# Two blocks of transformer layers in one kernel: another order of small matmuls between the large ones in the second block's mixer

## The chip, the cores and the metric

The kernel runs on one core of a Trainium2 chip. The time is the device time of one execution in microseconds (us), the median of three runs. A profiled execution gives the trace: spans of every instruction on TensorE (PE; its weight loads are shown apart as PEld), VectorE (DVE), ScalarE (ACT), GpSimd (POOL) and the DMA queues (SP).

## The reference

The input x (256 rows of 1024 values) goes through a first block and then a second block of two layers each. Each layer is a feed-forward part, a mixer and a second feed-forward part. Only the second block's mixer is touched. Cut to that:

```python
(z, xbc, dt_raw, rq, rk, rv, rg, aq, ak, av, gate) = jnp.split(h @ w_in[l], offsets, axis=-1)
y_ssd = ssd_mixer(z, xbc, dt_raw, ...)        # 16 heads of 64, chunks of 128 rows
y_ret = retention_mixer(rq, rk, rv, rg, ...)  # 4 heads
y_att = swa_sink_attention(aq, ak, av, ...)   # 16 query heads, 2 key/value heads, band of 256 keys
ys = jnp.stack([y_ssd, y_ret, y_att], axis=2)
branch = jnp.einsum('blmc,mcd->blmd', ys, w_branch[l])
gates = jax.nn.sigmoid((gate + b_gate[l]).reshape(bsz, L, N_BRANCH, D_MODEL))
y = jnp.sum(gates * branch, axis=2) @ w_out[l]

# in ssd_mixer, for each chunk and head j
lmat = jnp.exp(jnp.where(causal, seg, -jnp.inf))                       # the decays
y_diag = jnp.einsum('bcgjls,bcsgjp->bclgjp', cb[:, :, :, None] * lmat, xdt)
# in swa_sink_attention
p = e / (jnp.sum(e, axis=-1, keepdims=True) + jnp.exp(sink - m))
o = jnp.einsum('bnkgqs,bnskd->bnqkgd', p, vb)
```

## The kernel before, in words

Every engine has its own instruction queue, written out by hand in the order in which it executes; between the queues stand semaphores only. Nothing is scheduled by a tool.

**Units.** All weights stream through as units of 128x2048 values (`load`, on SyncE's queue, 5 buffers `raw`). ScalarE's `split` (line 1229) casts a unit to its high part `w_hi` (4 buffers), VectorE's `split` (line 1727) subtracts that and leaves the low part `w_lo`. TensorE's `product` (line 684) multiplies one 128x512 piece three times: high by high, high by low, low by high. One unit is used for both row blocks r = 0 and 1; `part` does one row block with one unit: 4 pieces x 3 = 12 products. The text calls that a half. `half(name, c, q, first, r)` is such a half for column chunk c of a projection, unit q of its two; `both` does r = 0 and 1; `chunk` does two units. Before a half TensorE waits until VectorE has split its unit (`unit_split`), and, where q is 0, until the accumulator pair that it overwrites was read (`chunk_read`, counted for r = 0 and 1 apart). A half that is done frees the unit (`unit_used`). ScalarE and VectorE interleave the splits with their own work by `through(u)`: split all units up to u of this mixer.

**Accumulators.** PSUM has four banks `acc`, used as two pairs (one bank for each row block), and four banks `work`, used in turn. The table `CHUNKS` gives each projection its pair: both chunks of gate_a (`gate_a0`, `gate_a1`) and both chunks of `gate_s` lie in pair 0; `ys`, the outputs of heads 0 to 7 and then of heads 8 to 15, lies in pair 1 both times. A bank of `work` is taken by `fill`, which waits until the last content was read (`work_read`).

**Attention.** For key/value group g and row block r, `attend` makes scores, VectorE masks them and takes maxima (lines 1966 to 1976), ScalarE makes the exponentials (line 1440) and scales them (line 1450), `turn_probs` transposes the four pairs of heads on TensorE into the four `work` banks (`probs_turned`, line 909), ScalarE copies them out (`copy_probs`, line 1467), and `gather` multiplies them with the values (`values`, line 925). Set (1, 0) has one key tile of 128 (8 transposes, 16 small products), set (1, 1) has two (16 and 32). ScalarE's `values_high` (line 1458) reads the result when both row blocks are in it. `add_bias` on VectorE (line 1948) scales a gate chunk from its accumulators, adds the bias and frees the pair.

**SSD heads.** ScalarE's `decays(i)` (lines 1669 and 1674) writes the decays of a group of heads, `HEADS = (0, 3, 6, 9, 12, 14, 16)`, into `seg`, which has six places: head hd uses place hd % 6, and so a group waits until the heads six before it are multiplied (`y_done`). VectorE's `weights` (line 2309) multiplies them with C·B, head by head (`seg_ready`). `weigh(hd)` on TensorE (lines 1181 and 1182) makes the head's output, 64 columns for each of two chunks. `carried` (line 1170) makes the part that comes from the first chunk's state; VectorE's `carry` (lines 2298 and 2301) takes it. VectorE's `skipped(g)` (line 2318) waits for the eight heads of group g, adds the skip and frees pair 1; `outputs(g)` (line 2331) multiplies with z. Beside these, TensorE runs the eight halves of `gate_s` (units 44 to 47).

The orders of ScalarE and VectorE around the heads, which the change does not touch:

```python
# ScalarE
decays(0); through(47); decays(1); decays(2); through(48)
decays(3); decays(4); through(49); gate(... "gate_s", 0 ...); decays(5); through(50)
# in decays(i), before the exponential that writes seg
if end > 6:
    act.wait_ge(y_done, l * 16 + (end - 6))
# VectorE
weights(range(0, 3)); through(47); weights(range(3, 6)); carry(0); carry(1); through(48)
add_bias(... "gate_s", 0 ..., rows=(0,)); weights(range(6, 8)); add_bias(..., rows=(1,))
skipped(0); weights(range(8, 11)); through(49); outputs(0); weights(range(11, 16))
skipped(1); outputs(1); through(50)
```

(The calls are put on fewer lines here, without their other arguments.)

Of the kernel before, what the change touches and what calls it, by code (L numbers as in the profile page):

```python
# [109 lines left out]
def build(nc, a):  # L110
# [3 lines left out]
    half = dm // 2  # L114
# [19 lines left out]
    with ExitStack() as ctx:  # L134
# [541 lines left out]
        def _(pe):  # L676
# [151 lines left out]
            def part(block, l, name, i, q, pos, r, x, kts=4, cols=512, units=2, turn_name=None):  # L828

                pair, n = count("chunks", block, l, name, i)  # L830
                if q == 0:
                    pe.wait_ge(chunk_read[pair], n * 2 - 1 + r)
                slot, nu = unit_count(pos)
                pe.wait_ge(unit_split[slot], nu + 1)
                for t in range(kts):
                    kt = kts * q + t
                    if turn_name and r == 0 and kt % 2 == 0:
                        turned(block, l, turn_name, kt // 2)
                    last = product(x[0], x[1], kt, r, pos, t * cols, cols, acc[2 * pair + r][:, 0:cols],
                                   kt == 0, q == units - 1 and t == kts - 1)  # L840
                last.then_inc(unit_used[slot], 1)
# [35 lines left out]
            def fill(block, l, name, i=0):  # L877

                bank, n = count("work", block, l, name, i)
                pe.wait_ge(work_read[bank], n)  # L880
                return work[bank], work_filled[bank]
# [19 lines left out]
            def probs_turned(block, l, g, r, e):  # L901

                nk = key_tiles(block, r)
                for hp in range(4):
                    bank, filled = fill(block, l, f"probsT{g}{r}", hp)
                    pe.wait_ge(probs_scaled, events(block, l, [8 * n for n in PASSES], 8 * g + 4 * r + hp + 1))
                    for s in range(2):
                        for kt in range(nk):
                            last = nc.tensor.transpose(bank[:, (s * nk + kt) * P:(s * nk + kt + 1) * P],  # L909
                                                       e(g, r, hp)[:, s, kt * P:(kt + 1) * P], ident[:, :])  # L910
                    last.then_inc(filled, 1)

            def values(block, l, g, r, e, v, kv):

                nk = key_tiles(block, r)
                pair, n = count("chunks", block, l, f"pv{g}")
                pe.wait_ge(chunk_read[pair], n * 2)
                for i in range(0, 4, 2):
                    for s in range(2):
                        turned(block, l, f"probsT{g}{r}", i + s)  # L920
                    for j in range(2):
                        for kt in range(nk):
                            for s in range(2):
                                pT = e(g, r, i + s).rearrange("p s n -> p (s n)")
                                last = nc.tensor.matmul(  # L925
                                    acc[2 * pair + i // 2][64 * s:64 * s + 64, j * 256 + r * P:j * 256 + (r + 1) * P],
                                    v[:, kt, kv(i) * 64:kv(i) * 64 + 64], pT[:, (j * nk + kt) * P:(j * nk + kt + 1) * P],
                                    start=kt == 0, stop=kt == nk - 1)
                    last.then_inc(pv_done, 1)
# [77 lines left out]
            def mixer2(l):  # L1007
# [13 lines left out]
                def half(name, c, q, first, r, x=xt, turn_name=None):  # L1021
                    part(1, l, name, c, q, m + first + q, r, x, turn_name=turn_name)

                def both(name, c, q, first, x=xt, turn_name=None):
                    for r in range(2):
                        half(name, c, q, first, r, x, turn_name)
# [34 lines left out]
                def turn_probs(g, r):  # L1061

                    probs_turned(1, l, g, r, B["e"])

                def gather(g, r):

                    values(1, l, g, r, B["e"], B["v"], lambda hp: g)
# [34 lines left out]
                attend(1, 1)  # L1102
                both("br_r", 1, 1, 24, yt)
                both("gate_a0", 0, 0, 26)
                turn_probs(1, 0)
                both("gate_a0", 0, 1, 26)
                gather(1, 0)
                turn_probs(1, 1)
                both("gate_a1", 0, 0, 28)
                gather(1, 1)  # L1110
                both("gate_a1", 0, 1, 28)
                chunk("xbc", 0, 30)
# [52 lines left out]
                def carried():  # L1165

                    pe.wait_ge(scaled_ready, l + 1)
                    for g in range(2):
                        bank, filled = fill(1, l, "mid", g)
                        nc.tensor.matmul(bank[:, :], S["cb"][:, g, 2 * P:3 * P], S["scaled"][:, g * 512:(g + 1) * 512],  # L1170
                                         start=True, stop=True).then_inc(filled, 1)

                def weigh(hd):

                    pair, n = count("chunks", 1, l, "ys", hd // 8)
                    if hd % 8 == 0:
                        pe.wait_ge(chunk_read[pair], n * 2)
                    pe.wait_ge(seg_ready, l * 16 + (hd + 1))
                    c, v = (hd % 8) * 64, slice(hd * 64, hd * 64 + 64)
                    w = S["seg"][:, hd % 6, :]  # L1180
                    nc.tensor.matmul(acc[2 * pair][:, c:c + 64], w[:, 0:P], S["xdt"][:, 0, v], start=True, stop=True)  # L1181
                    nc.tensor.matmul(acc[2 * pair + 1][:, c:c + 64], w[:, P:2 * P], S["xdt"][:, 1, v], start=True,  # L1182
                                     stop=True).then_inc(y_done, 1)

                def heads(hds):

                    for hd in hds:
                        weigh(hd)

                half("gate_s", 0, 0, 44, 0)  # L1190
                half("gate_s", 0, 0, 44, 1)
                carried()
                heads(range(0, 3))
                half("gate_s", 0, 1, 44, 0)
                heads(range(3, 6))
                half("gate_s", 0, 1, 44, 1)
                heads(range(6, 8))
                half("gate_s", 1, 0, 46, 0)
                heads(range(8, 11))
                half("gate_s", 1, 0, 46, 1)  # L1200
                heads(range(11, 16))
                half("gate_s", 1, 1, 46, 0)
# [1267 lines left out]
```

## Time and profile before

| | |
|---|---|
| median of 3 runs | 2458.09 us (2457.77 to 2458.26) |
| profiled execution | 2458.01 us, its span 2456.1 us |
| weight loads (PEld) | 83% busy |
| VectorE | 75% busy |
| ScalarE | 52% busy |
| GpSimd | 4% busy |
| DMA | 189 GB/s on average |

A row of a timeline reads: start in us, duration in us, engine, line, operation, what is written and what is read, and the number of instructions merged into the row; in brackets the idle time before it and the engine that ended it. The profile's ends of matmuls are modelled, and they overlap: two products that follow each other start 0.23 us apart though each is shown 0.39 us long. So costs on TensorE are read from start to start. fp32 products of the small kind appear as two instructions each.

The list of waits reads: engine and what it writes, line, the releasing instruction, total idle us, number of times, longest.

### The profile page before, as it was taken

The numbers are of one execution on the slowest core, as the hardware profiler recorded it, in microseconds if no ns is written. First come the engines' busy times: TensorE is split into PE (matmuls) and PEld (weight loads), VectorE is DVE, ScalarE is ACT, GpSimd is POOL, SyncE is SP. The second block draws the span as 40 slices with busy tenths as digits, with TensorE's granted clock in tenths as the row PEclk, the third lists the DMA queues.
The fourth block names the chain that finished last, engine by engine and source line by source line (L and its number), as shares of the span: only waits on it lengthen the run. The fifth ranks groups of instructions, "written<-read, shape, count | busy, mean of one in ns | idle before, by whom it ended". The sixth has DMA issues, their size and how long they took to land.

```text
span 2456.1 us, 30235 instructions
## 1 busy us (share of the span) xinstructions
PE 2443.5 (99%) x11626; PEld 2028.4 (83%) x11626; DVE 1852.8 (75%) x2898; ACT 1279.9 (52%) x1687; POOL 105.5 (4%) x128
## 2 busy tenths in 40 slices
PE   9999999999999999999999999999999999999999
PEld 7888888888888888788888888888888888888887
DVE  8775678778856788788657687877877657597876
ACT  5445654454457544544556665544544567564543
POOL 0000000000000000000100020000000100020000
PEclk9999999999999999999999999999999999999999
DMA  7675456555654556676654564665666644554663
GB/s 255 214 255 174 155 179 198 189 189 189 229 190 140 186 189 195 204 223 197 207 171 141 177 211 150 197 190 187 204 197 200 207 150 150 179 201 159 200 195 123
DMA packets 311390, 463.31 MB, mean 189 GB/s; under 512 B 18432, under 2 KB 208208, under 8 KB 310992
## 3 DMA queue, kind: packets, MB, share of 16 engines
q1 hardware_dynamic: 307280, 452.90, 56.9%
q10 hardware_dynamic: 3968, 8.49, 1.1%
q8 instruction: 93, 1.52, 0.2%
q14 instruction: 49, 0.40, 0.0%
HBM read 457.10 MB, written 4.23 MB: 188 GB/s over the span
## 4 chain that ended last, share of the span: by engine, by line
PE 98%; DMA 1%; ACT 1%; DVE 0%; SPq 0%; issue 0%; DVEq 0%; ACTq 0%
PE acc L684 53%; PE work L684 38%; PE work L691 1%; PE work L891 1%; PE acc L925 1%; PE work L909 1%; PE work L719 1%; DMA raw<-w_in_dram 0%; PE acc L1182 0%; PE work L1081 0%; DMA raw<-ffn_w_dram 0%; PE acc L1181 0%; PE acc L719 0%; PE work L962 0%; ACT w_hi L1229 0%; PE work L768 0%
## 5 line engine op out<-in xcount | busy, mean ns | idle before, releaser
L1727 DVE TENSOR_TENSOR w_lo<-raw,w_hi 128x2048 fp32r<-128x2048 f32 (+1 forms) x416 | 947.9, 2284 | 351.6 <-ACT w_hi L1229 348.9
L1229 ACT CAST w_hi<-raw 128x2048 fp32r<-128x2048 f32 (+1 forms) x416 | 788.2, 1904 | 302.9 <-PE acc L684 110.4
L684 PE MATMUL work<-w_hi,xt_hi 128*128 128x512 f32 x1408 | 549.0, 390 | 4.2 <-DVE xt_lo L1758 4.2
L684 PE MATMUL work<-w_hi,xt_lo 128*128 128x512 f32 x1408 | 548.0, 389 | 0.0
L684 PE MATMUL work<-w_lo,xt_hi 128*128 128x512 f32 x1408 | 547.9, 389 | 0.0
L684 PE MATMUL acc<-w_hi,yt_hi 128*128 128x512 f32 x1088 | 428.5, 394 | 0.0
L684 PE MATMUL acc<-w_hi,yt_lo 128*128 128x512 f32 x1088 | 424.0, 390 | 0.0
L684 PE MATMUL acc<-w_lo,yt_hi 128*128 128x512 f32 x1088 | 423.5, 389 | 0.0
L1887 DVE STREAM_TRANSPOSE field<-field 32x128 f32<-32x128 f32 x1280 | 387.7, 303 | 19.1
L684 PE MATMUL acc<-w_hi,xt_hi 128*128 128x512 f32 (+2 forms) x864 | 336.2, 389 | 0.0
L684 PE MATMUL acc<-w_hi,xt_lo 128*128 128x512 f32 (+2 forms) x864 | 330.4, 382 | 0.0
L684 PE MATMUL acc<-w_lo,xt_hi 128*128 128x512 f32 (+2 forms) x864 | 330.0, 382 | 0.0
L684 PEld LDWEIGHTS work<-w_hi,xt_hi 128*128 128x128 f32 x1408 | 264.3, 188 | 60.2 <-DVE w_lo L1734 3.7
L684 PEld LDWEIGHTS work<-w_hi,xt_lo 128*128 128x128 f32 x1408 | 264.3, 188 | 55.1
L684 PEld LDWEIGHTS work<-w_lo,xt_hi 128*128 128x128 f32 x1408 | 264.4, 188 | 54.5
L684 PEld LDWEIGHTS acc<-w_hi,yt_lo 128*128 128x128 f32 x1088 | 204.2, 188 | 43.4
L684 PEld LDWEIGHTS acc<-w_hi,yt_hi 128*128 128x128 f32 x1088 | 204.3, 188 | 42.4 <-issue 1.6
L684 PEld LDWEIGHTS acc<-w_lo,yt_hi 128*128 128x128 f32 x1088 | 204.5, 188 | 41.1
L1370 ACT CAST yt_hi<-field 128x512 fp32r<-128x512 f32 x80 | 49.8, 622 | 332.4 <-DVE field L1887 332.4
L1301 ACT ACTIVATE field<-work,rs 128x256 f32<-128x256 f32 x176 | 82.8, 474 | 208.1 <-PE work L684 207.7
L684 PEld LDWEIGHTS acc<-w_hi,xt_hi 128*128 128x128 f32 x864 | 162.5, 188 | 32.5 <-issue 2.7
L684 PEld LDWEIGHTS acc<-w_hi,xt_lo 128*128 128x128 f32 x864 | 162.3, 188 | 32.0
(182 smaller groups left out, 1641.6 us busy)
## 6 DMA issues: line engine op xcount, KB each, us to landing
raw<-ffn_w_dram SPq DMA_DIRECT2D x262, 512.0 KB, 4.5
raw<-w_in_dram SPq DMA_DIRECT2D x208, 512.0 KB, 4.5
raw<-w_ffn_in_dram SPq DMA_DIRECT2D x176, 512.0 KB, 4.7
raw<-w_ffn_out_dram SPq DMA_DIRECT2D x88, 512.0 KB, 4.3
raw<-w_branch_dram SPq DMA_DIRECT2D x48, 512.0 KB, 4.3
raw<-w_out_dram SPq DMA_DIRECT2D x32, 512.0 KB, 4.2
bias<-b_gate_dram SPq DMA_DIRECT2D x10, 512.0 KB, 7.7
raw<-w_branch_pool_dram SPq DMA_DIRECT2D x8, 512.0 KB, 4.2
```

The lines of the kernel that those rows point to most:

```text
L684: last = nc.tensor.matmul(out, x[:, kt, k], y, start=start and n == 0, stop=stop and n == 2)
L691: last = nc.tensor.transpose(work[bank][:, (2 * t + r) * P:(2 * t + r + 1) * P], src[:, r, c + t * P:c + (t + 1) * P], ident[:, :])
L719: last = nc.tensor.transpose(banks[pair][:, t * P:(t + 1) * P], h[:, r, kt * P:(kt + 1) * P], ident[:, :])
L891: last = nc.tensor.matmul(banks[s][0][:, j * 256:j * 256 + cols], q(i + j)[half_rows, r * P:(r + 1) * P], k(i + j)[half_rows, 0:cols], sta ...
L909: last = nc.tensor.transpose(bank[:, (s * nk + kt) * P:(s * nk + kt + 1) * P], e(g, r, hp)[:, s, kt * P:(kt + 1) * P], ident[:, :])
L925: last = nc.tensor.matmul(acc[2 * pair + i // 2][64 * s:64 * s + 64, j * 256 + r * P:j * 256 + (r + 1) * P], v[:, kt, kv(i) * 64:kv(i) * 6 ...
L1229: nc.scalar.copy(w_hi[:, slot, 0:n], raw[:, at, 0:n]).then_inc(hi_split[slot], 1)
L1301: nc.scalar.activation(act_gate[:, r, :], work[2 + r][:, 0:NARROW], ACT.Silu, scale=rs[:, r:r + 1]).then_inc(silu_ready, 1)
L1370: nc.scalar.copy(yt_hi[:, k:k + 2, :], hid_t).then_inc(hidden_hi, 1)
L1727: nc.vector.tensor_tensor(w_lo[:, at, 0:n], raw[:, at, 0:n], w_hi[:, slot, 0:n].bitcast(F32), ALU.subtract).then_inc(unit_split[slot], 1)
L1887: last = nc.vector.transpose(dst[:, :, :, 32 * i:32 * i + 32], src[:, :, :, 32 * o:32 * o + 32])
```

## The change

Only TensorE's order in the second block's mixer changes, in both of its layers. In the last attention, both transposed probability sets follow each other, behind the whole of gate_a0; and both products with the values follow each other, between the two units of gate_a1. Of the SSD heads, which stood in five groups (0 to 2 behind the carried part, 3 to 5, 6 and 7, 8 to 10, 11 to 15) between halves of gate_s, three groups remain: the carried part with heads 0 to 5, heads 6 to 10, heads 11 to 15.

```diff
                 attend(1, 1)
                 both("br_r", 1, 1, 24, yt)
                 both("gate_a0", 0, 0, 26)
+                both("gate_a0", 0, 1, 26)
                 turn_probs(1, 0)
-                both("gate_a0", 0, 1, 26)
-                gather(1, 0)
                 turn_probs(1, 1)
                 both("gate_a1", 0, 0, 28)
+                gather(1, 0)
                 gather(1, 1)
                 both("gate_a1", 0, 1, 28)
                 chunk("xbc", 0, 30)
...
                 half("gate_s", 0, 0, 44, 0)
                 half("gate_s", 0, 0, 44, 1)
+                half("gate_s", 0, 1, 44, 0)
                 carried()
-                heads(range(0, 3))
-                half("gate_s", 0, 1, 44, 0)
-                heads(range(3, 6))
+                heads(range(0, 6))
                 half("gate_s", 0, 1, 44, 1)
-                heads(range(6, 8))
                 half("gate_s", 1, 0, 46, 0)
-                heads(range(8, 11))
+                heads(range(6, 11))
                 half("gate_s", 1, 0, 46, 1)
                 heads(range(11, 16))
                 half("gate_s", 1, 1, 46, 0)
```

TensorE's instructions in order, the semaphores on which one waits in brackets. First the place around heads 6 to 10, in the first layer of the second block. Before: heads 6 and 7, and the half of gate chunk 1 behind them (its first two of twelve products).

```order
L684 MATMUL acc<-w_hi,xt_lo 128x512
L1181 MATMUL acc<-field 128x64 [waits seg_ready]
L1182 MATMUL acc<-field 128x64
L1181 MATMUL acc<-field 128x64 [waits seg_ready]
L1182 MATMUL acc<-field 128x64
L684 MATMUL acc<-w_hi,xt_hi 128x512 [waits unit_split1,chunk_read0]
L684 MATMUL acc<-w_lo,xt_hi 128x512
```

With the change the five heads stand together; the third, head 8, waits for pair 1 besides.

```order
L684 MATMUL acc<-w_hi,xt_lo 128x512
L1181 MATMUL acc<-field 128x64 [waits seg_ready]
L1182 MATMUL acc<-field 128x64
L1181 MATMUL acc<-field 128x64 [waits seg_ready]
L1182 MATMUL acc<-field 128x64
L1181 MATMUL acc<-field 128x64 [waits seg_ready,chunk_read1]
L1182 MATMUL acc<-field 128x64
L1181 MATMUL acc<-field 128x64 [waits seg_ready]
L1182 MATMUL acc<-field 128x64
L1181 MATMUL acc<-field 128x64 [waits seg_ready]
L1182 MATMUL acc<-field 128x64
L684 MATMUL acc<-w_hi,xt_hi 128x512 [waits unit_split1,chunk_read0]
```

The half that stood between head 7 and head 8 stands ahead of head 6 now.

The second place is the turning of the last two probability sets. Before: the first set (1, 0), and the half of gate_a0's second unit behind it.

```order
L909 MATMUL work<-ident,field 128x128 [waits probs_scaled,work_read1]
L909 MATMUL work<-ident,field 128x128
L909 MATMUL work<-ident,field 128x128 [waits probs_scaled,work_read2]
L909 MATMUL work<-ident,field 128x128
L909 MATMUL work<-ident,field 128x128 [waits probs_scaled,work_read3]
L909 MATMUL work<-ident,field 128x128
L909 MATMUL work<-ident,field 128x128 [waits probs_scaled,work_read0]
L909 MATMUL work<-ident,field 128x128
L684 MATMUL acc<-w_hi,xt_hi 128x512 [waits unit_split2]
```

With the change, from the last bank of the first set on: the second set goes into the same four banks, and the half of gate_a1 is next.

```order
L909 MATMUL work<-ident,field 128x128 [waits probs_scaled,work_read0]
L909 MATMUL work<-ident,field 128x128
L909 MATMUL work<-ident,field 128x128 [waits probs_scaled,work_read1]
L909 MATMUL work<-ident,field 128x128 x3
L909 MATMUL work<-ident,field 128x128 [waits probs_scaled,work_read2]
L909 MATMUL work<-ident,field 128x128 x3
L909 MATMUL work<-ident,field 128x128 [waits probs_scaled,work_read3]
L909 MATMUL work<-ident,field 128x128 x3
L909 MATMUL work<-ident,field 128x128 [waits probs_scaled,work_read0]
L909 MATMUL work<-ident,field 128x128 x3
L684 MATMUL acc<-w_hi,xt_hi 128x512 [waits unit_split3,chunk_read0]
```

The 24 products of gate_a0's second unit and the 16 small products of set (1, 0) no longer stand between the two sets.

## Rows read from the trace of the kernel before

**Rows 1.** The page, busy times and granted clock of TensorE in 40 slices.

```profile
PE 2443.5 (99%) x11626; PEld 2028.4 (83%) x11626; DVE 1852.8 (75%) x2898; ACT 1279.9 (52%) x1687; POOL 105.5 (4%) x128
...
PEclk9999999999999999999999999999999999999999
```

**Rows 2.** Waits of TensorE, whole program: the longest in total.

```profile
PE work L684 <- DVE xt_lo L1758: 4.2, 4, 2.1
```

**Rows 3.** Timeline of TensorE around the last attention, first layer.

```profile
1361.67 0.39 PE L684 MATMUL acc<-w_hi,xt_hi 128*128 128x512 f32 x1
...
1367.12 1.04 PE L909 MATMUL work<-ident,field 128*128 128x128 f32 x8
1367.91 0.47 PE L684 MATMUL acc<-w_hi,xt_hi 128*128 128x512 f32 x1
...
1373.57 1.09 PE L925 MATMUL acc<-field 128*64 128x128 f32 x16
1374.59 1.97 PE L909 MATMUL work<-ident,field 128*128 128x128 f32 x16
1376.32 0.47 PE L684 MATMUL acc<-w_hi,xt_hi 128*128 128x512 f32 x1
...
1381.98 1.97 PE L925 MATMUL acc<-field 128*64 128x128 f32 x32
1383.87 0.50 PE L684 MATMUL acc<-w_hi,xt_hi 128*128 128x512 f32 x1
```

**Rows 4.** Timeline of TensorE around the SSD heads, first layer.

```profile
1478.07 1.88 PE L1170 MATMUL work<-field 128*128 128x512 f32 x4
1479.78 0.33 PE L1181 MATMUL acc<-field 128*128 128x64 f32 x2
...
1481.04 0.48 PE L684 MATMUL acc<-w_hi,xt_hi 128*128 128x512 f32 x1
...
1483.89 0.33 PE L1181 MATMUL acc<-field 128*128 128x64 f32 x2
...
1488.00 0.33 PE L1181 MATMUL acc<-field 128*128 128x64 f32 x2
...
1495.77 0.33 PE L1181 MATMUL acc<-field 128*128 128x64 f32 x2
...
1497.91 0.48 PE L684 MATMUL acc<-w_hi,xt_hi 128*128 128x512 f32 x1
```

**Rows 5.** Timeline of all engines where TensorE waits for VectorE now.

```profile
1013.82 1.13 DVE L1758 SCALAR_TENSOR_TENSOR xt_lo<-work,vec,xt_hi 128x128 fp32r<-128x128 f32 x4 [0.64 <-ACT xt_hi L1293]
1014.54 0.19 PEld L684 LDWEIGHTS work<-w_hi,xt_hi 128*128 128x128 f32 x1 [0.89 <-issue]
1014.57 0.47 PE L684 MATMUL work<-w_hi,xt_hi 128*128 128x512 f32 x1 [0.68 <-DVE xt_lo L1758]
```

**Rows 6.** Timeline of ScalarE around the SSD heads: third group of decays, cast of unit 48.

```profile
1481.32 0.85 ACT L1674 ACTIVATE field<-after 128x768 f32<-128x768 f32 x1 [1.86 <-PE acc L1182]
1482.08 1.89 ACT L1229 CAST w_hi<-raw 128x2048 fp32r<-128x2048 f32 x1
```

**Rows 7.** Timeline of VectorE around the SSD heads.

```profile
1481.66 0.68 DVE L2298 TENSOR_TENSOR field<-work,sm 128x512 f32<-128x512 f32 x1
...
1484.31 2.28 DVE L1727 TENSOR_TENSOR w_lo<-raw,w_hi 128x2048 fp32r<-128x2048 f32 x1
1486.51 0.74 DVE L1948 SCALAR_TENSOR_TENSOR field<-acc,rs,bias 128x512 f32<-128x512 f32 x1
...
1489.11 1.29 DVE L2318 TENSOR_TENSOR field<-acc,field 128x512 f32<-128x512 f32 x2 [0.15 <-PE acc L1182]
1490.31 1.09 DVE L2309 TENSOR_TENSOR field<-field 128x256 f32<-128x256 f32 x3
...
1494.98 1.76 DVE L2309 TENSOR_TENSOR field<-field 128x256 f32<-128x256 f32 x5
```

**Rows 8.** Timeline of ScalarE in the last attention: copies of set (1, 0).

```profile
1372.49 1.16 ACT L1467 COPY field<-work 128x256 f32<-128x256 f32 x4
```

**Rows 9.** Timeline of VectorE there, last attention: split of unit 29, bias addition of gate_a0.

```profile
1372.62 2.29 DVE L1727 TENSOR_TENSOR w_lo<-raw,w_hi 128x2048 fp32r<-128x2048 f32 x1 [1.85 <-ACT w_hi L1229]
1374.83 1.40 DVE L1948 SCALAR_TENSOR_TENSOR field<-acc,rs,bias 128x512 f32<-128x512 f32 x2
```

## The prediction

> **What bounds the kernel now.** I read the page's busy times first: TensorE is busy 2443.5 of 2456.1 us, and its granted clock is 0.9 or more in every slice [rows 1]. The list of waits then says that TensorE idles almost nowhere for another engine: the largest entry is 4.2 us over four places, all at stage starts [rows 2]. So the span is TensorE's own queue, and two things alone can change it: how densely its instructions follow each other, and new waits in that queue. The change alters no instruction, only their order, so I lay the timeline of TensorE over those of ScalarE and VectorE at the two places. In what follows a time is the start of a row; "+2.31" is measured from the start of head 6. A half is twelve 512-column products. In a long run the pitch is 0.227 us (24 of them from 1361.67 to 1367.12 [rows 3]), so an uninterrupted half is 2.72 us; the first half behind small fp32 work takes 2.85 us (1481.04 to 1483.89 [rows 4]).
>
> **What the merging saves, if nobody waits.** Heads: three cost 1.26 us (1479.78 to 1481.04) and five 2.14 us (1495.77 to 1497.91) [rows 4], 0.44 us for each more head, so six cost 2.58 us. From 1478.07 the stretch up to the end of head 15 takes 19.84 us now. After the change it is 2.72 (half) + 1.71 (carried, 1478.07 to 1479.78) + 2.58 + 2.85 + 2.72 + 2.14 + 2.85 + 2.14 = 19.71 us: 0.13 us less. Attention: from 1367.12 to 1383.87 is 16.75 us now [rows 3]. After it is 5.45 (24 uninterrupted products) + 0.79 + 1.73 (8 and 16 transposes) + 5.66 (24 products behind them, 1367.91 to 1373.57) + 2.77 (48 small products; 16 cost 1.02 and 32 cost 1.89, so 0.88 more for 16 more) = 16.40 us: 0.35 us less. All of it would be 0.48 us a layer, 0.96 us for both.
>
> **How long a released TensorE needs.** VectorE's four-instruction group starts at 1013.82 and lasts 1.13 us; the second, which TensorE needs, is done some 0.60 us in, at 1014.42. The product starts at 1014.57 [rows 5]: I add 0.15 us to the end of each releasing instruction. The weight load starts only at 1014.54, so here it was not pulled ahead of the wait. The Trainium skill, "TensorE: Matmul & The Clock Gate", section "Architectural detail: the array is 16× 32×32, not 1× 128×128", says that TensorE's queue can pull weight loads ahead of matmuls in flight. By that rule a restart could be about 0.12 us cheaper, and the forecast below, with five restarts a layer, 1.2 us lower; the row speaks against it for a load behind a wait.
>
> **Heads, wait A (first half of gate chunk 1).** That half overwrites the accumulator which VectorE's first bias addition reads. The addition stands behind VectorE's split of unit 48, that behind ScalarE's cast of unit 48, and that in ScalarE's queue behind the third group of decays, which waits until heads 0 to 2 are done, since it reuses their buffers. Now heads start at 1479.78, the decays' exponential at 1481.32 (+1.54) and the cast 0.76 later [rows 6]. The change starts heads at 1478.07 + 2.72 + 1.71 = 1482.50. So: exponential 1484.04, cast 1484.80, done 1486.69 (1.89 long), split of VectorE from 1486.72, addition 2.20 behind it at 1488.92 (as 1484.31 to 1486.51 [rows 7]), done 0.74 later at 1489.66, TensorE free at 1489.81. Unhindered it arrives at 1482.50 + 2.58 + 2.85 = 1487.93. A is 1.88 us. The carried products, moved behind a half as well, are no second term: VectorE reads them at 1481.66 now and could from about 1481.85 then, long before the split at 1486.72.
>
> **Heads, wait B (head 8).** Head 8 is the first to overwrite the accumulators that heads 0 to 7 filled. VectorE empties them with two additions, which wait for head 7, and only behind these multiplies the weights of head 8. Today a half lies between heads 7 and 8; the change puts head 8 right behind head 7. With head 6 at 1488.00 [rows 4], the additions start at +1.11 and the weights at +2.31 [rows 7]. Three weights take 1.09 us and five 1.76 us, so the first is done 0.42 us after its start. TensorE goes on at +2.31 + 0.42 + 0.15 = +2.88; it stands there at +0.88. B is 2.00 us, whatever VectorE did before, since both additions hang on head 7.
>
> **Heads, wait C (head 11).** Behind B come 1.26 us of heads and a half of 2.85 us: +6.99. VectorE's chain from head 7 (additions, three weights, split of unit 49, outputs) is the same as now and reaches the next weights at 1494.98, that is +6.98; the first is ready for TensorE at +6.98 + 0.42 + 0.15 = +7.55. C is 0.56 us. Five heads of 2.14 us end the stretch at +9.69. With A, head 6 stands at 1489.81 + 2.72 = 1492.53, and the stretch ends at 1502.22 instead of 1497.91: **+4.31 us** a layer.
>
> **Attention, waits T and G.** The 16 transposes of the second set reuse the four banks of the first set, which ScalarE must have copied. TensorE fills the first bank from 1372.57 and it is done some 0.4 us later; a copy of 128x256 lasts under 0.4 us (four take 1.16 us [rows 8]); with 0.15 us TensorE goes on at about 1373.51 instead of 1373.36: T is 0.15 us, and the other banks are ahead. Next, gate chunk 1 overwrites what the bias addition of chunk 0 reads. That addition starts at 1374.83 because VectorE splits a unit before it [rows 9], and that split hangs on ScalarE's work on probabilities, which TensorE's order does not touch. Done at 1375.57, TensorE goes on at 1375.72; it stands there at 1373.51 + 1.73 = 1375.24: G is 0.48 us. Together −0.35 + 0.15 + 0.48 = **+0.28 us** a layer. Now the 16 small products and 16 transposes cover the addition; that cover is what the edit removes. The first set's products with the values come 24 products later and the second set's stay where they are; ScalarE reads the results of both only when the second's are there, so nobody waits longer for that move.
>
> **Sum.** Nothing behind absorbs this, since TensorE has no slack to give up [rows 2]. ScalarE's and VectorE's later splits, and the raw loads on SyncE's queue, wait for units that TensorE frees, so they shift along. No GpSimd instruction stands between these places. Two layers: 2 x (4.31 + 0.28) = 9.2 us on the profiled execution's 2458.01 us: **2467.2 us**, also against the median of 2458.09 us, which is 0.08 away.
>
> **Rivals.** (1) **A is hidden**: the chain through the cast of unit 48 is shorter than I add, or ScalarE's exponential runs ahead. For it: six steps are chained, and each is taken from one row. Against it: 1.88 us would have to vanish. Then head 6 starts at 1490.65, the stretch ends at 1500.34, and the price is 2 x (2.43 + 0.28) = 5.4 us: 2463.4 us. (2) **Not slower**: the mechanism is the order of VectorE and ScalarE. If their reads of the accumulators were ready whenever TensorE arrives, only the removed switches would be left, and the time would be 2458.01 − 0.96 = 2457.1 us. It decides where B falls under 0.2 us, that is if the weight of head 8 were multiplied before head 7 ends. For it: TensorE waits for almost nothing now [rows 2], in a kernel with many such hand-overs. Against it: the additions in front of that weight themselves wait for head 7, which no slack changes. (3) **The clock falls** behind the new idle stretches. Now it is full with idle stretches of 0.68 us [rows 1, 5], but none of 2 us is in the trace after the start. If the half behind A and the one behind B ran at 1.2 instead of 2.4 GHz, each would take about 2.7 us more, 10.9 us for both layers: 2478.1 us. The Trainium skill, same page, section "A second HAM failure mode: psum-queue depth-cycling", reports a kernel whose clock swings because TensorE idles briefly between groups while it goes round PSUM banks; nothing in this trace shows that. That the change doesn't do what it says is excluded by the order of instructions.
>
> **How the numbers follow.** Forecast 0.78, rival (1) 0.10, rival (2) 0.09, rival (3) 0.03. The bounds of the unknown costs: a restart costs 0.03 to 0.3 us, five a layer but not additive, about ±1.0 us; a releasing step in each chain may be off by 0.3 us, four times over both layers, ±1.2 us. Forecast's own range is so 2465 to 2469.5 us. The range reaches down to rival (1) and leaves out the others: 2463.0 to 2470.0 us. A measurement of this kernel tells 0.2% (4.9 us) from no change. Slower by more takes the forecast, the clock and half of rival (1): 0.86. Within 0.2%: the other half of (1) and most of (2): 0.12. Faster: 0.02.
>
> **What would show it.** In the new profile: TensorE's waits, four or five new ones a layer, on head 8 (for VectorE's weights) about 2.0 us, on the first product of gate chunk 1 (for VectorE's bias addition) about 1.9 us, on head 11 about 0.6 us, and in the attention about 0.5 us; ScalarE's cast of unit 48 some 2.7 us later against the start of the stretch; a granted clock still at 1.00. I am wrong if TensorE runs through heads 7 and 8 without a gap, if the time lost is found outside these two stretches, or if the halves take 5.4 us.

## The result, and the profile after

The changed kernel takes 2473.03 us (median of six runs, 2469.90 to 2475.14); before took 2458.18 us in the same runs (2457.64 to 2458.62). The ratio is 1.0059, 95% interval 1.0049 to 1.0069: slower, by 14.9 us, where 9.2 us were forecast. The direction was right, the size wrong, and the time lies outside the range. A second thing changed besides the median: the six executions spread over 5.2 us, where those of before spread over 1.0 us.

| | before | after |
|---|---|---|
| profiled execution, its span | 2458.01, 2456.1 us | 2473.57, 2470.8 us |
| TensorE busy | 2443.5 us | 2450.2 us |
| mean granted clock | 0.999 | 0.997 |

TensorE's waits in the whole program, after (to [rows 2]): the first row was there before (4.2 us), the second and third are new.

```profile
PE work L684 <- DVE xt_lo L1756: 4.5, 4, 2.2
PE acc L684 <- DVE field L1946: 4.0, 4, 1.9
PE acc L1181 <- DVE field L2307: 3.7, 2, 1.9
```

New waits of 7.7 us do not make 14.7 us of span, and TensorE is even 6.7 us longer busy with the same instructions. The timeline of TensorE around the heads (to [rows 4]) shows both parts; the last two rows are the same two waits in the second layer:

```profile
1478.34 0.39 PE L684 MATMUL acc<-w_hi,xt_hi 128*128 128x512 f32 x1
...
1481.06 1.88 PE L1170 MATMUL work<-field 128*128 128x512 f32 x4
...
1488.00 0.39 PE L684 MATMUL acc<-w_hi,xt_lo 128*128 128x512 f32 x1
1490.00 0.50 PE L684 MATMUL acc<-w_hi,xt_hi 128*128 128x512 f32 x1 [1.62 <-DVE field L1946]
...
1492.88 0.33 PE L1181 MATMUL acc<-field 128*128 128x64 f32 x2
...
1493.49 0.39 PE L1182 MATMUL acc<-field 128*128 128x64 f32 x2
1495.75 0.41 PE L1181 MATMUL acc<-field 128*128 128x64 f32 x2 [1.88 <-DVE field L2307]
...
1497.09 0.75 PE L684 MATMUL acc<-w_hi,xt_hi 128*128 128x512 f32 x1
1497.63 0.63 PE L684 MATMUL acc<-w_lo,xt_hi 128*128 128x512 f32 x1
1498.06 0.63 PE L684 MATMUL acc<-w_hi,xt_lo 128*128 128x512 f32 x1
...
1501.52 0.33 PE L1181 MATMUL acc<-field 128*128 128x64 f32 x2
...
1503.67 0.48 PE L684 MATMUL acc<-w_hi,xt_hi 128*128 128x512 f32 x1
...
2213.71 0.63 PE L684 MATMUL acc<-w_hi,xt_hi 128*128 128x512 f32 x1 [1.90 <-DVE field L1946]
...
2221.03 0.66 PE L1181 MATMUL acc<-field 128*128 128x64 f32 x2 [1.87 <-DVE field L2307]
```

Wait A stands ahead of the product at 1490.00, wait B ahead of head 8 at 1495.75. Behind B the heads still run at the pace of before; from the half at 1497.09 on, 1.3 us after the wait has ended, the products follow each other 0.43 us apart instead of 0.23 us. The granted clock in windows (columns: window, its length, TensorE's busy time and instructions, granted clock, share of DMA, GB/s), first layer and then second:

```profile
1490.00:1493.00 3.00, 3.00 (x14) 1.00 0.84 321
1493.00:1496.00 3.00, 1.12 (x12) 1.00 0.00 0
1496.00:1498.00 2.00, 2.00 (x14) 0.78 0.00 0
1498.00:1500.00 2.00, 2.00 (x6) 0.50 0.00 0
1500.00:1502.00 2.00, 2.00 (x11) 0.87 0.00 0
2213.70:2217.00 3.30, 3.29 (x8) 0.53 0.72 270
2217.00:2221.00 4.00, 2.16 (x13) 0.93 0.00 0
2221.00:2227.50 6.50, 6.47 (x21) 0.50 0.00 0
```

0.50 is 1.2 GHz, 1.00 is 2.4 GHz; a value between them is a window that holds both. In the first layer the clock fell behind B alone; in the second it fell behind A, rose, and fell again behind B. Before the change it stood at 1.00 through both places. The page's line of 40 slices hides this: every digit is still a 9, as in [rows 1].

VectorE and ScalarE around A (to [rows 6, 7]):

```profile
1484.32 0.84 ACT L1672 ACTIVATE field<-after 128x768 f32<-128x768 f32 x1 [4.57 <-PE acc L1182]
1485.07 1.89 ACT L1227 CAST w_hi<-raw 128x2048 fp32r<-128x2048 f32 x1
```

```profile
1486.99 2.29 DVE L1725 TENSOR_TENSOR w_lo<-raw,w_hi 128x2048 fp32r<-128x2048 f32 x1 [2.13 <-ACT w_hi L1227]
1489.20 0.74 DVE L1946 SCALAR_TENSOR_TENSOR field<-acc,rs,bias 128x512 f32<-128x512 f32 x1
...
1493.98 1.29 DVE L2316 TENSOR_TENSOR field<-acc,field 128x512 f32<-128x512 f32 x2 [2.71 <-PE acc L1182]
1495.19 1.09 DVE L2307 TENSOR_TENSOR field<-field 128x256 f32<-128x256 f32 x3
```

This is the chain as the prediction wrote it: decays at 1484.32, cast at 1485.07, split at 1486.99, addition at 1489.20; the trace runs 0.27 us behind that of before when the stretch begins, and with that each start in this first layer is within 0.03 us of the forecast. The attention (to [rows 3]) came as forecast too:

```profile
1372.61 2.81 PE L909 MATMUL work<-ident,field 128*128 128x128 f32 x24
1375.69 0.50 PE L684 MATMUL acc<-w_hi,xt_hi 128*128 128x512 f32 x1 [0.27 <-DVE field L1946]
...
1384.17 0.50 PE L684 MATMUL acc<-w_hi,xt_hi 128*128 128x512 f32 x1
```

### The profile page after: what moved, and what is told of

Its sections match the earlier page's. It is cut to its first block, busy times and chain, and to the rows that moved or that the text cites. A ratio compares the mean times of both kernels' runs of the same rounds, so it can differ in the third digit from the quotient of the medians.

```text
span 2470.8 us, 30235 instructions
## 1 busy us (share of the span) xinstructions
PE 2450.2 (99%) x11626; PEld 2033.5 (82%) x11626; DVE 1853.3 (75%) x2898; ACT 1280.2 (52%) x1687; POOL 105.4 (4%) x128
## 4 chain that ended last, share of the span: by engine, by line
PE 96%; ACT 1%; DVE 1%; DMA 1%; issue 1%; POOL 0%; SPq 0%; DVEq 0%; ACTq 0%
PE acc L684 52%; PE work L684 38%; PE work L691 1%; PE acc L925 1%; PE work L891 1%; PE work L719 1%; PE work L909 0%; ACT w_hi L1227 0%; DMA raw<-w_in_dram 0%; ACT field L1438 0%; PE work L1081 0%; DMA raw<-ffn_w_dram 0%; PE acc L1181 0%; PE acc L1182 0%; PE acc L719 0%
```

## The experiments

After the result two theories stood against each other. **Mine**: the waits cost what the prediction says (9.2 us), and the remaining 5 to 6 us are TensorE at half clock behind them. **The rival**: the slow products have another cause (the start after a wait, memory traffic), or the waits alone count. The first four runs take the change apart, the others take away the idleness, or the cause of a wait. Each run is compared with executions of before that were measured together with it.

**Heads alone.** The change with the attention put back.

```diff
                 both("gate_a0", 0, 0, 26)
-                both("gate_a0", 0, 1, 26)
                 turn_probs(1, 0)
+                both("gate_a0", 0, 1, 26)
+                gather(1, 0)
                 turn_probs(1, 1)
                 both("gate_a1", 0, 0, 28)
-                gather(1, 0)
                 gather(1, 1)
```

> The SSD heads in the change's three groups, the attention in the order of before. My theory: nearly all of the loss is in the heads, as waits of TensorE (4.1 us a layer) and, behind them, products at half clock. In the profiled execution of the change the heads cost 5.5 us in the first layer and 8.8 us in the second, the attention 0.24 us in each. So about 2472.5 us, granted clock below 1.00 behind the waits. Rival (the waits alone count, what the clock shows costs nothing): 2466.8 us.

Measured: 2472.9 us (2469.79 to 2474.2), before 2457.86 us, ratio 1.0058 (1.0043 to 1.0073). Practically the whole loss is in the heads. The rival's 2466.8 us is out.

**Attention alone.** The change with the heads put back.

> The attention's sets turned and multiplied together, the heads in the order of before. My theory: 2 x 0.28 us more, one wait of about 0.3 to 0.5 us a layer on the first product of gate_a1, clock at 1.00: 2458.7 us. Rival (a short wait already brings the clock down, about 1.7 us each time): up to 2462 us and a clock under 1.00 near 1376 us.

Measured: 2458.55 us against 2457.86 us, ratio 1.0003 (0.9993 to 1.0012), clock 1.00 around the place. The waits of 0.3 us did not bring the clock down in its profile. The forecast of 2458.7 us fits, but 0.7 us more is not told from no change by these runs.

```profile
PE acc L684 <- DVE field L1948: 0.5, 2, 0.3
```

**The first six heads alone.**

```diff
                 half("gate_s", 0, 0, 44, 1)
+                half("gate_s", 0, 1, 44, 0)
                 carried()
-                heads(range(0, 3))
-                half("gate_s", 0, 1, 44, 0)
-                heads(range(3, 6))
+                heads(range(0, 6))
                 half("gate_s", 0, 1, 44, 1)
```

> Only the carried part and heads 0 to 5 are put together, heads 6 and 7 and heads 8 to 10 stay apart with a half between. The bias addition behind the late cast of unit 48 now holds up the weights of head 6: one wait of about 2.2 us a layer before head 6, 2 x 2.15 us more than before: 2462.4 us if the clock stays full. If one idle stretch of 2 us is enough for the clock to fall, some 1.7 us more for each fall: up to 2466 us, more scatter between runs. Rival (head 8 is the only costly wait): 2458.0 us.

Measured: 2466.86 us (2462.66 to 2468.32), before 2457.86 us, ratio 1.0032 (1.0021 to 1.0042). The wait is where and as long as expected, and the clock falls behind it in both layers of the profiled execution (clock 0.57 over 4 us behind the first):

```profile
PE acc L1181 <- DVE field L2308: 4.2, 2, 2.2
...
1491.00:1495.00 4.00, 4.00 (x13) 0.57 0.37 135
```

The single executions say more than the median. The two whose mean clock was 1.000 took 2462.66 and 2463.36 us, where 2462.4 us were worked out for a full clock; the three at 0.998 took 2464.30 to 2467.14 us, and the three at 0.997 took 2467.68 to 2468.32 us. The same program with the same wait has both. The median lies 0.9 us above the 2466 us that were expected as the upper end: in the profiled execution the fall cost some 1.6 us in the first layer, as assumed, but some 3.1 us in the second, where the products ran at half clock from 2211.91 to 2218.48 (that layer's stretch took 25.34 us, 5.49 us over before, of which about 2.4 us are the wait).

**Heads 6 to 10 alone.**

```diff
                 half("gate_s", 0, 1, 44, 1)
-                heads(range(6, 8))
                 half("gate_s", 1, 0, 46, 0)
-                heads(range(8, 11))
+                heads(range(6, 11))
```

> Only heads 6 to 10 are put together, behind the half that stood between heads 7 and 8; the carried part and heads 0 to 5 as before. One wait of about 2.0 us a layer at head 8 and one of 0.5 us at head 11: 2 x 2.5 us more, 2463.1 us at full clock. If a single idle stretch brings the clock down: up to 2466.5 us, and the wait at head 11 gone. Rival (the wait before gate chunk 1 is the only costly one): 2458.0 us.

Measured: 2465.3 us (2462.29 to 2466.99), before 2457.86 us, ratio 1.0029 (1.0018 to 1.004). Again the wait is the expected one (3.8 us in two places, the longest 1.9 us shown), and again the two executions at a mean clock of 1.000 (2462.29 and 2463.06 us) are those that the sum of waits gives (2463.1 us). The profiled one ran at half clock from 1494 to 1501:

```profile
1494.00:1501.00 7.00, 7.00 (x23) 0.52 0.00 0
```

**TensorE kept busy while it waits.** The change, with seven products of 512 columns into a bank of `work` that nobody needs then, in each of the two waits. They add work and compute nothing that is used.

```diff
+                def keep_busy(n):
+                    bank, filled = count("work", 1, l, "turn_s", 0)
+                    pe.wait_ge(work_read[bank], filled)
+                    for _ in range(n):
+                        nc.tensor.matmul(work[bank][:, :], xt_hi[:, 0, 0:P],
+                                         xt_hi[:, 0:2, :].rearrange("p k n -> p (k n)"), start=True, stop=True)
...
                 half("gate_s", 0, 1, 44, 1)
+                keep_busy(7)
                 half("gate_s", 1, 0, 46, 0)
-                heads(range(6, 11))
+                heads(range(6, 8))
+                keep_busy(7)
+                heads(range(8, 11))
```

> The change, with seven extra products of 512 columns in each of the two idle stretches of TensorE (ahead of gate chunk 1's first half and ahead of head 8), into a work bank that is free there; they take 1.6 us, less than the wait. My theory (the loss beyond 9.2 us is the clock that falls when TensorE idles): the releases come when they came, the clock stays at 1.00, the time drops by some 5 us to about 2467.3 us, with the small scatter of before. Rival (the slow products behind the waits have another cause, such as the released engine's own start, or memory traffic): no gain, 2473 us or more.

Measured: 2467.44 us (2467.22 to 2468.41), before 2458.5 us, ratio 1.0036 (1.0024 to 1.0049). With 28 more products in the program the loss against before falls from 14.9 to 8.9 us (the medians differ by 5.6 us), to the forecast made from the waits alone, and the spread between runs is 1.2 us again. The timeline shows the same releases, all some 0.57 us earlier because the whole stretch begins that much earlier in this trace, with the wait filled. Head 11 now waits too (the row at 1499.73), since no slow half hides its wait:

```profile
1487.65 1.75 PE L1196 MATMUL work<-xt_hi 128*128 128x512 f32 x7
1489.43 0.50 PE L684 MATMUL acc<-w_hi,xt_hi 128*128 128x512 f32 x1
...
1493.09 1.87 PE L1196 MATMUL work<-xt_hi 128*128 128x512 f32 x7
1495.16 0.41 PE L1181 MATMUL acc<-field 128*128 128x64 f32 x2 [0.20 <-DVE field L2319]
...
1499.73 0.43 PE L1181 MATMUL acc<-field 128*128 128x64 f32 x2 [0.24 <-DVE field L2319]
...
1501.98 0.48 PE L684 MATMUL acc<-w_hi,xt_hi 128*128 128x512 f32 x1
```

The clock in all windows of the stretch is 1.00, as here behind the second filled wait:

```profile
1496.00:1500.00 4.00, 3.76 (x22) 1.00 0.00 0
```

That is the test of the cause: the kernel is the change with the added products and the wait for their bank, the releases come when they came, the idleness goes, and with it the excess. Against the rival's two other causes speaks the trace of the change itself. In its first layer the product behind B and those of heads 8 to 10 ran at full pace for 1.3 us before the slow ones began, so it is not the engine's start after a wait. And no DMA ran in the slow windows from 1496 to 1502, while the products from 1490 to 1493 kept clock 1.00 at a DMA share of 0.84, so it is not memory traffic.

**Kept busy ahead of head 8 only.** The same without the first `keep_busy(7)`.

> The same, but only the stretch ahead of head 8 is filled. My theory: the clock can still fall behind the first wait (gate chunk 1), where the change showed it in the second layer and not in the first: between 2467.3 and 2471 us, with scatter. Rival (only the second of two near idle stretches brings the clock down): 2467.3 us, no fall.

Measured: 2469.42 us (2468.32 to 2470.95), before 2458.5 us, ratio 1.0044 (1.0029 to 1.0059). In the profiled execution the clock holds behind wait A in the first layer and falls in the second, as in the change itself:

```profile
2212.00:2216.00 4.00, 3.50 (x9) 0.63 0.72 251
```

So one idle stretch is enough, and it needs no earlier one nearby.

**Cast of unit 48 first.** The change, with ScalarE's order mended.

```diff
                 decays(1)
-                decays(2)
                 through(48)
+                decays(2)
```

> The change, with ScalarE's cast of unit 48 ahead of the third group of decays, so that VectorE's split and the bias addition need not wait for heads 0 to 2. My theory: the wait ahead of gate chunk 1 is gone, that at head 8 stays at 2.0 us and brings the clock down as in the run with heads 6 to 10 alone: 2463.4 us at full clock, about 2466 us with one fall a layer. Rival (the addition is late for another reason): the wait stays, 2473 us.

Measured: 2466.57 us (2464.02 to 2468.98), before 2458.5 us, ratio 1.0032 (1.0021 to 1.0043). Wait A is gone; on the first product of a gate chunk only the attention's is left:

```profile
PE acc L1181 <- DVE field L2307: 4.2, 4, 1.9
...
PE acc L684 <- DVE field L1946: 0.5, 2, 0.3
```

The profiled execution is the fastest of the seven, 2464.02 us: its clock stayed at 1.00 behind both waits of 1.88 us at head 8, and the sum gave 2463.4 us for that.

Put together, the profiled executions in which such a wait stands unfilled (the change, heads alone, first six, heads 6 to 10, kept busy ahead of head 8, and this one) hold thirteen waits of 1.87 to 2.23 us and three of 1.61 or 1.62 us. Behind eleven of the thirteen the clock fell, at once or up to 1.6 us later; the two here are the exceptions. Behind the three shorter ones, each the wait A of a first layer, it stayed at 1.00 until the next wait. No run varied the length alone, so whether the length decides is not shown.

**Cast first, waits at head 8 avoided.** The run with the first six heads, with the cast moved as above.

> Carried part and heads 0 to 5 together, heads 6 and 7 and heads 8 to 10 apart, attention as before, and the cast of unit 48 ahead of the third group of decays: both causes of waiting are away. My theory: no new wait, clock at 1.00, 0.1 us less than before in each layer: 2457.7 us, no difference from before. Rival (the merging itself costs): above 2459 us.

Measured: 2458.08 us against 2458.5 us, ratio 0.9998 (0.9989 to 1.0008). No new wait is left. From 1478.41 to the end of head 15 at 1498.20 is 19.79 us; before it was 19.84 us [rows 4]; in the second layer it is 19.80 against 19.85 us. So in the traces merging as such costs nothing, and gains 0.05 us in each layer where one group fewer stands between the halves. The times can't show so little.

**Bias addition first, attention alone.** The attention as changed, the heads as before, and VectorE's order mended.

```diff
-                through(29)
                 dve.wait_ge(bias_loaded[1], events(1, l, (16, 16), 16))
                 add_bias(1, l, "gate_a0", 0, m + 27, B["gate"][:, :, 0:512], 1, 0)
+                through(29)
```

> The attention in the order of the change with the bias addition ahead of the split of unit 29; the heads wholly as before. My theory: the wait of 0.3 to 0.5 us on gate_a1 is gone, the stretch from the first set's place to the end of the products with the values is about 0.2 us shorter than before in each layer: 2457.7 us. Rival (the wait stays since the copies of the first set are what holds): 2458.6 us as with the attention alone.

Measured: 2457.85 us against 2458.09 us, ratio 1.0 (0.9991 to 1.0008). No wait is left in the attention. The time is not told from no change; the gain is read from the trace. In its profile the 24 transposes start at 1372.16 and the next large product of the following half, behind the values, at 1383.14:

```profile
1372.16 2.81 PE L909 MATMUL work<-ident,field 128*128 128x128 f32 x24
...
1380.37 2.84 PE L925 MATMUL acc<-field 128*64 128x128 f32 x48
```

With the 5.45 us of the 24 products ahead that is 16.43 us, where before took 16.75 us [rows 3] and the change 17.01 us: 0.32 us gained a layer, almost the 0.35 us of the switches.

**Cast first, and kept busy ahead of head 8.**

> The change with the cast of unit 48 first (no wait ahead of gate chunk 1) and seven extra products in the idle stretch ahead of head 8. My theory: only the 2.0 us at head 8 and 0.5 us at head 11 and the attention's 0.24 us remain, at full clock: 2 x (2.43 + 0.24) = 5.3 us over before, 2463.6 us, scatter as small as before. Rival (the clock falls for another reason than idleness): 2466.6 us as with the cast moved alone.

Measured: 2464.06 us (2463.33 to 2464.67), before 2458.09 us, ratio 1.0023 (1.0014 to 1.0033). The sum gave 2463.6 us. Without the seven products the same order took 2466.57 us against 2458.5 us, a loss of 8.1 us where 6.0 us are left here. In the profile the clock is 1.00 in every window behind the waits: its fall is taken out, waits B and C remain.

**Everything that pays, together.** First six heads together, cast first, heads 6 to 7 and 8 to 10 apart, attention as changed, bias addition first.

> Carried part and heads 0 to 5 together, heads 6 and 7 and heads 8 to 10 apart, cast of unit 48 ahead of the third group of decays; the attention in the order of the change, and VectorE's bias addition of gate_a0 ahead of its split of unit 29, so that gate_a1 need not wait for it. My theory: no wait over 0.2 us is left in either place, the saved switches remain, 0.13 us a layer in the heads and 0.35 less 0.15 us in the attention: 0.7 us under before, 2457.4 us, which the trace can show and the times hardly. Rival (moving the addition makes the split of unit 29 late for gate_a1's second unit): a new wait there, 2458 us or more.

Measured: 2457.07 us (2456.83 to 2458.54) against 2458.09 us, ratio 0.9997, interval 0.9988 to 1.0006. No wait in either place is left, but 1.0 us in the medians is not told from no change by these runs. It is 16 us better than the change, and not shown to be better than before.

## Why the prediction was wrong, step by step

- **The switches** (0.13 and 0.35 us a layer less). Small, and right as far as shown: 0.32 us in the attention, once its wait was gone, and 0.05 us in the heads for one of the two groups that are saved. The 0.13 us was not measured by itself.
- **Wait A, 1.88 us.** In the change the last product ahead of it starts at 1488.00 and the next at 1490.00: 2.00 less 0.23 us of pitch is 1.77 us; in the second layer it is 2213.71 less 2211.43 less 0.23, 2.05 us. The chain behind it was right in every link in the first layer, and moving the cast took the wait away in both.
- **Wait B, 2.00 us.** From 1493.49 to 1495.75, less 0.22 us, is 2.04 us, and the same in the second layer.
- **Wait C, 0.56 us.** At full clock, in the run with TensorE kept busy, head 11 starts 7.44 us behind head 6 (1492.29 to 1499.73), where 7.55 us were forecast. In the change the slow half covers the wait: head 11 is late by the clock and no longer by VectorE.
- **Heads in all, +4.31 us a layer.** With TensorE kept busy the first layer's stretch ends 24.21 us after its start (1477.77 to 1501.98), 4.37 us over before.
- **Attention, +0.28 us.** 17.01 less 16.75 is 0.26 us. Within it T was too large: the 24 transposes and the switch behind them took 2.56 us in the run without wait G, where 2.52 us were worked out without any wait, so T is about 0.04 us instead of 0.15 us.
- **The restart, 0.15 us.** It held behind weights of a head (0.42 us after 1495.19 is 1495.61, TensorE starts at 1495.75: 0.14 us) and was too long behind the bias additions (1489.94 to 1490.00: 0.06 us). The weight load of the product released at 1490.00 starts at the same 1490.00, and that of head 8 at 1495.72, so here too none was pulled ahead of the wait.
- **The sum of waits, 9.2 us.** With TensorE kept busy the loss is 8.9 us. This sum was right.
- **Rival (3), the clock, at a chance of 0.03: the step that failed.** The sum put the clock at full behind every new wait and so at no cost. What it had for this was a full clock behind an idle stretch of 0.68 us; the prediction itself says that none of 2 us is in the trace after the start (at the start there is one, 2.14 us ahead of the product at 9.36, with clock 1.00 behind it). It still gave the fall 0.03 and left the case with the largest price out of the range. The runs showed half clock behind most of the waits of 1.87 us and more. It does not come each time: one fall in the first layer and two in the second in the profiled execution.
- **What the fall cost.** The first layer's stretch took 5.49 us more than before (1478.34 to 1503.67 is 25.33 us), of which 4.31 are the waits forecast; the half at 1497.09 took 4.43 instead of 2.85 us, which is 1.58 us, less the 0.5 us of wait C that it covers. In the second layer the half behind A took 1.6 us more, and heads 8 to 10 with the half behind them 3.1 us more; its stretch, 2201.77 to 2230.43, took 8.81 us more than before. With 0.26 us of attention in each layer that makes 14.8 us, and the span grew by 14.7 us. The rival's price, 2478.1 us with both halves of both layers wholly at half clock, was not reached (2475.14 us at most): the halves took 4.4 to 4.7 us and not the 5.4 us that were named as a sign of being wrong, since the clock came back before the end of each, but heads 8 to 10 could run slowly as well, which the price left out.
- **The Trainium skill**, "TensorE: Matmul & The Clock Gate", section "A second HAM failure mode: psum-queue depth-cycling", tells of a kernel that loses time because brief idle stretches between groups make the clock swing. By that rule the forecast should have held a loss beyond the waits. The traces agree that brief idle stretches make the clock swing, with windows at 0.50 to 0.57 behind waits of 1.87 to 2.23 us; here the waits come from the order of VectorE's work, not from going round the banks. The case was given too small a chance.

What is open: why the same wait leaves the clock alone in one execution and not in the next. Runs with one wait of about 2 us a layer show both. Nor is it shown why the clock stays down for some 3 us behind one wait and over 6 us behind another.

## What to carry to other kernels

Small matmuls put between large ones of a queue that waits for nothing are not only switches: each large piece between them is time in which the other engines free a buffer and prepare the next operand. Before merging them, write down for each waiting instruction who must finish first and where that stands in its own queue. And where TensorE runs dense at full clock, price a new wait of 2 us at more than its length, because the products behind it may run at half clock: here it cost between its own length and some 2.3 times as much (5.5 us for a wait of about 2.4 us). Filling the wait with products that nobody uses took that part back.

## What the runs showed of the hardware that was not expected

- One idle stretch of TensorE of 1.87 to 2.23 us brought the granted clock to 0.50 behind eleven of thirteen such waits, and left it at 1.00 behind two, of 1.88 us. Both happen in one program: 2462.66 us and 2468.32 us are two executions of the run with the first six heads alone, mean clock 1.000 and 0.997. Three stretches of 1.61 or 1.62 us and those of 0.3 us in the attention left it alone in every window read.
- The fall need not follow at once: behind wait B in the first layer the clock was full for 1.3 us after TensorE had started again.
- A fall cost about 1.6 us (a half of 2.85 us took 4.43 us), and about 3.1 us where heads and the half behind them ran slowly.
- Twenty-eight products that nobody uses made the kernel 5.6 us faster (medians 2473.03 and 2467.44 us, each with its own runs of before at 2458.18 and 2458.5 us).
